# Expert stage of a one-core backbone layer: gathers written out, thirteen row slots for eight, weights made rank by rank

## What is computed

```python
q = (xb @ w_query).reshape(PEER_BLOCK, PEER_HEADS, 2, PEER_QDIM // 2)
s = jnp.einsum('thpd,hpnd->thpn', q, sub_keys)
sv, si = lax.top_k(s, PEER_TOPK)
...
top_s, pos = lax.top_k(cand, PEER_TOPK)
idx = jnp.take_along_axis(cidx, pos, axis=-1)
gate = jax.nn.softmax(top_s.astype(jnp.float32), axis=-1)
act = jax.nn.gelu(jnp.einsum('thkd,td->thk', expert_u[idx], xb).astype(jnp.float32))
return jnp.einsum('thk,thkd->td', (gate * act).astype(xb.dtype), expert_v[idx])
```

## Time and profile before

| | |
|---|---|
| Median of 3 runs | 2315.96 us (2307.59 to 2316.02) |
| Profiled execution, span from first to last instruction | 2306.0 us |
| PE busy | 1797.9 us, 78% |
| DVE busy | 1125.9 us, 49% |
| POOL busy | 1040.6 us, 45% |
| ACT busy | 269.0 us, 12% |
| Bytes moved | 723.11 MB, mean 314 GB/s |

### The profile page before, as it was taken

One profiled execution on the slowest core, in us unless ns is written; L12 is line 12 of the kernel. 1 busy time (PEld: TensorE's weight loads), 2 busy tenths in 40 slices (PEclk: granted clock), 3 DMA queues, 4 the chain that ended last, 5 costly groups with the idle time before them and its releaser, 6 DMA issues.

```text
span 2306.0 us, 17408 instructions
## 1 busy us (share of the span) xinstructions
PE 1797.9 (78%) x4545; PEld 809.9 (35%) x4545; DVE 1125.9 (49%) x1856; ACT 269.0 (12%) x629; POOL 1040.6 (45%) x1089
## 2 busy tenths in 40 slices
PE   7979999999698995766676777767767767677776
PEld 1124544555344882222222322222222222222232
DVE  0136787233354465545545545545455456354433
ACT  0120101112101001101101011011011010110111
POOL 1000000000000157666676676676766766767752
PEclk9999999999898997899999899999999898998999
DMA  7887877331674598999899999999999999999986
GB/s 278 324 295 275 298 266 269 110 110 56 255 261 176 189 358 326 367 373 362 341 381 373 369 373 369 368 367 372 364 366 370 368 373 372 365 382 372 367 331 252
DMA packets 144196, 723.11 MB, mean 314 GB/s; under 512 B 10121, under 2 KB 10329, under 8 KB 77090
## 3 DMA queue, kind: packets, MB, share of 16 engines
q0 software_dynamic: 92784, 614.83, 69.6%
q1 hardware_dynamic: 51216, 107.78, 13.1%
q10 hardware_dynamic: 162, 0.08, 0.0%
HBM read 720.52 MB, written 2.13 MB: 313 GB/s over the span
## 4 chain that ended last, share of the span: by engine, by line
POOL 33%; PE 28%; issue 17%; DMA 14%; DVE 4%; POOLq 3%; ACT 1%; DVEq 0%; ACTq 0%; SPq 0%
POOL ring L357 20%; POOL wg L354 13%; PE ps L703 10%; DMA ring<-in_expert_u,wg 5%; PE ps L829 4%; DMA ring<-in_expert_v,wg 3%; DMA ring<-in_w_mod 3%; PE ps L651 3%; PE ps L697 2%; PE ps L893 2%; DMA ring<-in_w_out 1%; PE ps L866 1%; PE ps L756 1%; DMA ring<-in_w_in 1%; POOLq L354 1%
## 5 line engine op out<-in xcount | busy, mean ns | idle before, releaser
L893 PE MATMUL ps<-ring,wg 128*128 128x512 f32 x2000 | 999.6, 649 | 414.3 <-DMA ring<-in_expert_v,wg 412.9
L1261 DVE SCALAR_TENSOR_TENSOR ring<-ring,A 128x2048 f32<-128x2048 f32 x256 | 584.5, 2295 | 649.6 <-DMA ring<-in_expert_u,wg 641.4
L893 PEld LDWEIGHTS ps<-ring,wg 128*128 128x128 f32 x2000 | 393.8, 206 | 1020.1 <-issue 698.5
L357 POOL DMA_INDIRECT ring<-in_expert_v,wg x256 | 334.9, 1308 | 209.5 <-POOL wg L354 187.5
L357 POOL DMA_INDIRECT ring<-in_expert_u,wg x256 | 327.3, 1279 | 199.4 <-POOL wg L354 176.9
L354 POOL COPY wg<-acc 128x1 uint32 x512 | 333.4, 651 | 140.0 <-DVE ring L1261 61.2
L593 ACT ACTIVATE wg<-K,VX 128x128 f32<-128x128 f32 x250 | 97.2, 401 | 1258.3 <-PE ps L893 992.0
L703 PE MATMUL ps<-ring,H 128*128 128x512 f32 x512 | 225.0, 598 | 5.0 <-DMA ring<-in_w_in 3.8
L304 POOL DMA_DIRECT2D ring<-in_w_mod x32 | 28.6, 892 | 398.3 <-DVE acc L922 290.2
L922 DVE SCALAR_TENSOR_TENSOR acc<-ring,vec,acc 128x512 f32<-128x512 f32 x240 | 180.5, 752 | 13.5 <-DMA ring<-in_w_mod 5.2
L703 PEld LDWEIGHTS ps<-ring,H 128*128 128x128 f32 x512 | 96.8, 191 | 130.0 <-issue 123.2
(11 more groups left out here) (207 smaller groups left out, 920.3 us busy)
## 6 DMA issues: line engine op xcount, KB each, us to landing
ring<-in_w_mod POOLq DMA_DIRECT2D x32, 2048.0 KB, 8.9
ring<-in_w_mod SPq DMA_DIRECT2D x16, 2048.0 KB, 7.9
ring<-in_w_in SPq DMA_DIRECT2D x16, 2048.0 KB, 11.5
ring<-in_w_out SPq DMA_DIRECT2D x8, 2048.0 KB, 13.9
ring<-in_w_query SPq DMA_DIRECT2D x8, 2048.0 KB, 13.1
ring<-in_expert_u,wg POOLq DMA_INDIRECT x256, 8.4
ring<-in_expert_v,wg POOLq DMA_INDIRECT x256, 8.8
B<-in_ctx SPq DMA_DIRECT2D x2, 1024.0 KB, 10.7
```

What stands on the lines that cost most here:

```text
L357: nc.gpsimd.indirect_dma_start(ring[:, slot, :], None, table, bass.IndirectOffsetOnAxis(ap=index, axis=0)).then_inc(loaded, 16)
L893: ins = mm(ps[:, 4 * b + n, :], diag[:, s, :], ring[:, s, n * CH:(n + 1) * CH], start=False, stop=False, skip_group_check=True)
L1261: v.scalar_tensor_tensor(out=ring[:, 4 + s, :], in0=ring[:, 4 + s, :], scalar=1.0, in1=A[:, b, :], op0=ALU.mult, op1=ALU.mult, accum_out=d ...
```

## The change

- **Gathers.** The loops are written out, and the gather reads its row numbers from `eidx` itself. The copy, its semaphore and the wait are gone.
- **Slots.** Tiles that are dead in the expert stage become places for rows: U has six (four of `ring`, the modulation row's place in `VX`, and `qh`), V has seven (four of `ring`, two in `H`, and `modrow`). The first 20 U gathers go alone with five places, since `qh` is still in use.
- **Order.** V of rank r follows U of rank r+4 (before: r+24). To get there, sixteen rounds issue one U and two V each. The V gathers begin when PE has computed all scores.
- **Weights.** ACT makes gelu, product and diagonal for each rank as its dot ends. DVE only divides a group's exponentials by their sum, before the ninth dot of the group ahead of it.
- **PE.** It takes all 256 ranks, and the first matmul of a bank clears it.
- **End.** Block 0 is added, scaled and stored during block 1's ranks. Block 1 goes in quarters of 512 columns, each when its bank is done.

The diff, cut to its core; what it removes beyond the lines shown is the code printed above.

```diff
-LAG = TOPK + TOPK // 2
-TAIL_SLOT = 1
...
+RANKS = TB * PH * TOPK
+BLOCK_RANKS = PH * TOPK
+EARLY = 5
+LEAD = 20
+LAG = 4
+U_SLOTS, V_SLOTS = 6, 7
...
+def u_slot(r):
+    return r % EARLY if r < LEAD else (r - LEAD) % U_SLOTS
+U_BEFORE = [max((p for p in range(r) if u_slot(p) == u_slot(r)), default=None) for r in range(RANKS)]
+U_LOADS = [sum(u_slot(p) == u_slot(r) for p in range(r + 1)) for r in range(RANKS)]
...
+        u_rows = [*(ring[:, 4 + i, :] for i in range(4)), VXf[:, 0:D],
+                  qh[:].rearrange("p a b t -> p (a b t)")]
+        v_rows = [*(ring[:, i, :] for i in range(4)), Hf[:, 0:D], Hf[:, D:2 * D], modrow[:]]
         wgf = flat(wg)
         diag = wgf[:, 0:4 * P].rearrange("p (s n) -> p s n", s=4)
...
-            def gather(table, slot, rank, index, count, loaded):
-                nc.gpsimd.tensor_copy(index, eidx[:, bass.ds(rank, 1)]).then_inc(S["copied"], 1)
-                pool.wait_ge(S["copied"], count)
-                pool.nop(nofuse=True)
+            def gather(table, rows_, rank, loaded):
                 nc.gpsimd.indirect_dma_start(
-                    ring[:, slot, :], None, table, bass.IndirectOffsetOnAxis(ap=index, axis=0)
+                    rows_, None, table,
+                    bass.IndirectOffsetOnAxis(ap=eidx[:, rank:rank + 1], axis=0)
                 ).then_inc(loaded, 16)
...
+            def gather_u(r):
+                if r % TOPK == 0:
+                    pool.wait_ge(S["picked"], r // TOPK + 1)
+                if U_BEFORE[r] is not None:
+                    pool.wait_ge(S["u_free"], U_BEFORE[r] + 1)
+                gather(expert_u[0], u_rows[u_slot(r)], r, u_ld[u_slot(r)])
+            def gather_v(r):
+                if r >= V_SLOTS:
+                    pool.wait_ge(S["pair_free"], r - V_SLOTS + 1)
+                gather(expert_v[0], v_rows[r % V_SLOTS], r, v_ld[r % V_SLOTS])
...
+            pool.wait_ge(S["h2_ready"], 2 * TB)
+            for r in range(LEAD):
+                gather_u(r)
             pool.wait_ge(S["w_free"], 48)
...
-                pool.nop(nofuse=True)
...
+            pool.wait_ge(S["score_psum"], 8)
+            for i in range(LEAD - LAG):
+                gather_u(LEAD + i)
+                gather_v(2 * i)
+                gather_v(2 * i + 1)
+            for r in range(2 * (LEAD - LAG), RANKS - LAG):
+                gather_u(r + LAG)
+                gather_v(r)
...
+            for r in range(RANKS - LAG, RANKS):
+                gather_v(r)
...
+            def soft_of(g):
+                act.wait_ge(S["picked"], g + 1)
+                nc_a.activation(soft[:, g * TOPK:(g + 1) * TOPK], topd[:, g * TOPK:(g + 1) * TOPK],
+                                ACT.Exp, accum_out=sums[:, g:g + 1]).then_inc(S["exp_ready"], 1)
...
+                if n == 2:
+                    soft_of(0)
+                    soft_of(1)
...
+            def weight_of(r):
+                act.wait_ge(S["u_free"], r + 1)
+                link(nc_a.activation(act_t[:, r:r + 1], dots[:, r:r + 1], ACT.Gelu_apprx_tanh))
+                link(nc_a.activation(wgt[:, r:r + 1], act_t[:, r:r + 1], ACT.Copy,
+                                     scale=soft[:, r:r + 1]))
+                if r >= 4:
+                    act.wait_ge(S["pair_free"], r - 3)
+                nc_a.activation(diag[:, r % 4, :], ident, ACT.Copy, scale=wgt[:, r:r + 1]
...
+            def final_std(b):
+                for n in range(4):
+                    act.wait_ge(S["ssq3"], 4 * b + n + 1)
+                    cols = slice(n * CH, (n + 1) * CH)
+                    ins = nc_a.activation(A[:, b, cols], B[:, b, cols], ACT.Square,
+                                          accum_out=st[:, 8 + n:9 + n])
                 link(ins)
...
+                link(nc_a.activation(st[:, 16:20], st[:, 8:12], ACT.Identity, scale=1.0 / D,
+                                     accum_out=st[:, b:b + 1]))
+                nc_a.activation(st[:, 2 + b:3 + b], st[:, b:b + 1], ACT.Sqrt, bias=eps
                                 ).then_inc(S["std3"], 1)
+            for g in range(TB * PH):
+                act.wait_ge(S["soft_ready"], g + 1)
+                for r in range(g * TOPK, (g + 1) * TOPK):
+                    weight_of(r)
+                    if r % TOPK == 3 and 2 <= g + 1 < TB * PH:
+                        soft_of(g + 1)
+                if g == PH + 1:
+                    final_std(0)
+            link(nc_a.activation(st[:, 20:21], eps, ACT.Sqrt))
+            final_std(1)
...
+            for r in range(RANKS):
+                b, k = r // BLOCK_RANKS, r % BLOCK_RANKS
+                pe.wait_ge(S["diag_ready"], r + 1)
+                pe.wait_ge(v_ld[r % V_SLOTS], 16 * (r // V_SLOTS + 1))
                 for n in range(4):
-                    ins = mm(ps[:, 4 * b + n, :], zeros, K[:, 0:CH], start=True, stop=True)
...
+                    ins = mm(ps[:, 4 * b + n, :], diag[:, r % 4, :],
+                             v_rows[r % V_SLOTS][:, n * CH:(n + 1) * CH],
+                             start=k == 0, stop=k == BLOCK_RANKS - 1, skip_group_check=True)
+                    if r == RANKS - 1:
+                        ins.then_inc(S["bank_done"], 1)
+                if r < RANKS - 1:
                     ins.then_inc(S["pair_free"], 1)
...
+            def norm_soft(g):
+                dve.wait_ge(S["exp_ready"], g + 1)
+                link(v.reciprocal(sums[:, g:g + 1], sums[:, g:g + 1]))
+                cols = slice(g * TOPK, (g + 1) * TOPK)
+                v.tensor_scalar(soft[:, cols], soft[:, cols], sums[:, g:g + 1], None, ALU.mult
+                                ).then_inc(S["soft_ready"], 1)
+            def dot(r):
+                rows_u = u_rows[u_slot(r)]
+                dve.wait_ge(u_ld[u_slot(r)], 16 * U_LOADS[r])
                 v.scalar_tensor_tensor(
...
+                    out=rows_u, in0=rows_u, scalar=1.0, in1=A[:, r // BLOCK_RANKS, :],
+                    op0=ALU.mult, op1=ALU.mult, accum_out=dots[:, r:r + 1]
+                ).then_inc(S["u_free"], 1)
+            def add_peer(b):
...
+                for n in range(4):
+                    if b == 0:
+                        dve.wait_ge(S["pair_free"], BLOCK_RANKS)
+                    else:
+                        dve.wait_ge(S["bank_done"], n + 1)
+                    cols = slice(n * CH, (n + 1) * CH)
+                    bank = ps[:, 4 * b + n, :]
+                    link(v.tensor_tensor(bank, bank, ga2[:, cols], ALU.mult))
+                    v.tensor_tensor(B[:, b, cols], B[:, b, cols], bank, ALU.add
+                                    ).then_inc(S["ssq3"], 1)
+            def final_norm(b):
+                dve.wait_ge(S["std3"], b + 1)
+                link(v.reciprocal(st[:, 4 + b:5 + b], st[:, 2 + b:3 + b]))
+                for n in range(4):
+                    cols = slice(n * CH, (n + 1) * CH)
+                    v.scalar_tensor_tensor(out=B[:, b, cols], in0=B[:, b, cols],
+                                           scalar=st[:, 4 + b:5 + b], in1=gy[:, cols],
+                                           op0=ALU.mult, op1=ALU.mult
+                                           ).then_inc(S["final_ready"], 1)
...
+            for g in range(TB * PH):
+                for r in range(TOPK):
+                    if g == 0 and r == TOPK // 2:
+                        dve.wait_ge(S["score_ready"], 3)
+                        pick(2, 2)
+                    if g == 1 and r == LEAD - TOPK:
+                        dve.wait_ge(S["score_ready"], 8)
+                        norm_soft(0)
+                        norm_soft(1)
+                    if 2 <= g + 1 < TB * PH and r == TOPK // 2:
+                        norm_soft(g + 1)
+                    dot(g * TOPK + r)
+                if 3 <= g + 2 < TB * PH:
                     pick(g + 2, g + 2)
...
+                if g == PH + 1:
                     dve.wait_ge(S["ld_ga2"], 16)
                     add_peer(0)
...
+                if g == PH + 2:
+                    dve.wait_ge(S["ld_gfin"], 16)
+                    final_norm(0)
```

More of the change, by code:

```diff
@@ L359, in gather @@
                 ).then_inc(loaded, 16)
[L361 to L373, removed]
@@ L376, in _ @@
[L376 to L382, removed]
-            pool.wait_ge(S["w_free"], 48)
[L384 to L387, removed]
-                pool.nop(nofuse=True)
-                with pool.Fori(0, hq) as q:
-                    pairs(q, g * TOPK + q * 4 + TOPK, g * (2 * TOPK) + q * 8 + (LAG - TOPK))
@@ L1212, in pick @@
                 sq = lambda t: t.rearrange("p (a c) -> p a c", a=TOPK)
[L1213 removed]
+                step(v.tensor_copy(stage, sc[:, g * (2 * NK):(g + 1) * (2 * NK)]))
                 for p_ in range(2):
@@ L1250, in dot @@
-            def dot(g, b, first=False):
-                for r in range(TOPK):
-                    s = r % 4
-                    if r == TOPK // 2 and not first:
-                        weights(g - 1, g)
-                    if r == 8 and first:
```

(45 more changed lines are left out.)

121 lines of the change are left out of this document (11 added, 110 removed).

## The result

The changed kernel takes **2139.8 us** (median of four runs, 2136.2 to 2143.1), the kernel before, run beside it, 2315.0: a ratio of 0.9256, 95% interval 0.9234 to 0.9277. 2132 was forecast, in a range of 2100 to 2210. The profiled execution has a span of 2137.8 us, 2 us under its median.

The account below looks back on a forecast made before the run. POOL's serial issue was taken as the bound. 871.2 + 2 (first landing) + 492 x 2.497 + 3 (U 30) + 2.5 (stores) + 15 (end) = 2122 us span, plus 10 to the median = 2132 us; range 2100 to 2210.

Parts of the forecast that it names:

- The bound: Expert stage: POOL's serial issue of copies and gathers sets the pace, 5.44 us of a 5.75 us U and V pair.
- Slots: Expert stage: with 13 slots for 8, 30 us of queued transfers outlast the dots' longest stop, 14.6 us, once 20.
- V 4 ranks behind: Expert stage: weight due 20 us after its U's landing; it takes 6 us, 19 with a pick, 24 once.
- ScalarE: Expert stage: weights made rank by rank take 1.3 us a rank, at most 2.5, where 5 us are available.
- Rate: Expert stage: a deep queue carries 420 GB/s, 2.497 us a gather, with 492 gathers left after the scores.
- Start: Before the V gathers: TensorE and w_query's loads set it; last score copy ends at 871.2 as before, V starts at once.
- End: After the last landing: about 15 us to the end of the span, 20.8 before; no V is late.
- U 30: Expert stage, group 1: the wait for exponentials makes this U gather some 3 us too late for a full queue: +3.
- A: Rival, expert stage: each pair still waits out one dot, 2.62 us a gather, span 2183, time 2193; chance 0.20.
- B: Rival, expert stage: transfers already at their limit, only start and end change, 2300 to 2320 us; chance 0.04.
- C: Rival, expert stage: TensorE stays at half clock, 6.75 us a rank, time about 2630 us; chance 0.05.
- The condition set at the prediction's end: Expert stage: prediction wrong if fast stretches were fast because dots had stopped, not because the queue was full.

Follow-up runs that it names:

- LAG 12: The changed kernel with V gathers 12 ranks behind U instead of 4: 2221.0 us, ratio 0.9608 to the kernel before.

## Why the prediction was right, and where it was off

**The bound.** Right: POOL's serial chain was the bound. With the copies back it fills all the time and the windows fall to 361 to 396 GB/s; without them landings lead the chain. A gather then costs POOL 2.8 us: a copy of 0.59, 0.82 of wait and a gather of 1.40. Free of DVE's holds it would be 0.19, 0.82 and 0.94, 1.95 us by an estimate from these rows; without the wait it is 1.97 (0.49, 0.15 and 1.33, by the run with unwaited copies). Both are under the 2.48 us of the transfers. So neither the wait nor the holds would have made POOL the bound alone. That the wait was needed for it is shown; that the holds were is this sum, and no run took them away.

**Slots.** Right that 30 us of queue cover a pick, and eight do worse. The prediction gave the 13 slots one argument; only the two more for U count (with the fifth early one), and about half of their 34 us is the single stop at 950, where it had looked at picks.

**V 4 ranks behind.** Right in that no weight was late: behind the scores nearly all of TensorE's idle time is put down to landings of V (299 us), and none to a diagonal. What the short distance buys was not seen. The prediction took the wait for the exponentials as a cost of group 1 alone. In group 1 it came, at 957.5 for 943, later by what the start was later, and cost 2 us (406 GB/s for 50 us) where 3 were taken. DVE itself stood 39 us there. In the groups behind, LAG 4 keeps the wait away; LAG 12 shows it.

**ScalarE.** 0.87 us a rank for the 1.3 taken. Its own time was on no path; its order was, through the exponentials.

**Rate.** 423 GB/s, 2.479 us a gather, for 420 and 2.497: 492 of them give 8.9 us less.

**Start: the step that failed.** "TensorE and w_query's loads set it" was right, and that it would end at 871.2 as before was not. The copies had spaced the gathers ahead of the scores, so removing them made the 2 MB pieces of `w_query` later: 22.2 us from issue to landing in the median between 780 and 890 us, 17.6 before and 17.0 with the copies back. TensorE waited 3.2 us for the same piece with them back and 10.9 without. The scores end at 872.1 with copies and 888.6 without where the slots are four and four, and at 876.5 and 886.3 with 13.

The 15.1 us are 2.0 by which the queries begin later (746.6 for 744.6, ahead of any gather, so no part of this), 10.5 of wait and 2.6 of matmuls at the lower clock behind it. Nothing is transferred in the time that they add, as the 20 gathers ahead are through. The prediction counted what the faster POOL issues in the stage, and not what it collides with ahead of it.

**End.** 15 us from the last landing were taken, and the flow ebbs from 2114 on (53 GB/s, then 10): from 2114.1 to the end it is 23.7, 8.7 more. Two things are in this. One DMA engine lags: the landing events of the trace have the last V complete on fourteen of 16 engines at 2115.1 and on the last at 2120.3. And TensorE is behind: V gathers land 2.48 us apart once no U is left between them (2112.9, 2115.4, 2117.8, 2120.3), a rank takes 3.47, and the last rank starts near 2124.5, 4.2 us behind its landing and 13.3 before the end. The prediction had TensorE take the last V as it lands.

**The sum again:** 2122 + 15.1 (start) - 8.9 (rate) - 1 (U 30) + 8.7 (end) = 2135.9, against a span of 2137.8. The forecast put the median 10 us over the span; here it is 2. A run's time lies some 2 us over its own span in both kernels (2307.59 for 2306.0, 2139.44 for 2137.8); the other 8 came in because the profiled execution of the kernel before was its fastest. So 8 us of miss are 16 of span less 8 of offset: two errors that partly hide each other, and the closeness of 2132 is in part luck.

**The rivals.** A (POOL stays the bound, 2183) needed every pair to wait out a dot; while it catches up, one gather of three does. B (a ceiling at 374) is refuted by 423 GB/s over 1,100 us: the ceiling was POOL's. The Trainium skill (HBM Reference, Specifications (TRN2)) has both numbers, about 358 as a core's share and about 425 for a core that streams alone; the windows agree with the second. C (half clock): the granted clock is 0.98 to 1.00 with TensorE idle a quarter of the time, higher than the 0.93 of the earlier trace rows. The condition set at the prediction's end, that the fast stretches were fast because the dots had stopped, does not hold either.

## What to carry to other kernels

When every window of a stage has the same rate, ask the chain of waits who is late before calling it a ceiling, and count a small instruction with the semaphore behind it and what holds it: a copy of 0.19 us, the 0.8 us of wait behind it and DVE's holds, ahead of each gather, were 5.9 of the 7.4 points. When an issuing engine gets faster, look at what its transfers will now run ahead of: here loads that TensorE needed, at a price of some 13 us. More gathers ahead, behind a wait for those loads, won 16 us. Buffers pay where the longest stop is, so find out which side's slots empty the queue before giving memory to both.

## What the runs showed of the hardware

- A full queue of 8 KB rows carries 423 GB/s without a break for 1,100 us, though each gather takes 25 to 26 us from issue to landing (the page's medians), as there are some ten in front of it.
- A plain load shares with gathers in flight: the median of four 2 MB pieces went from 17.6 to 22.2 us when the gathers came closer together, was 17.0 with the copies back, and 15.2 where gathers waited for pieces.
- A gather's issue of 0.94 us takes up to 3.0 when a dot is running on DVE, and ends some 0.8 us behind it (1256.96 for a dot that ends at 1256.15). The Trainium skill (Advanced Engine Details and Errata, GPSIMD Details) says that GpSimd and VectorE share ports and conflict when a VectorE instruction has two SBUF inputs, as the dot has; the timeline agrees. No run tried a dot with one such input.
- At the end of the queue the last 8 us carry a trickle. Slices of the changed kernel, 2112 to 2123 us:

```profile
GB/s 328 328 268 298 298 238 238 149 119 30 60 60 60 60 30 60 60 30 30 30 30 30 30 30 0 30 30 30 0 0 0 0 0 0 0 0 0 0 0 0
```

30 GB/s is about what one of 16 engines carries of 424 (26.5), so one or two of them run behind the rest; the last V's landing events put the slowest 5.2 us behind the fourteenth. Which it is, and why, is not known.
